# Hybrid decoder step: paced page gathers, one product for the rotary scores, four row groups for the mLSTM outer products, another start and end

## The reference

```
h = RMSNorm(x); z = h @ w_in
branch A: gated DeltaNet, 4 heads, chunked, state S per sample
branch B: latent attention, 8 heads; a sample reads 2048 past rows
          (128 latent + 32 rotary values) from pages of a page table:
          s = (q_lat . c_past + q_rope . k_past) * scale; softmax; ctx = p . c_past
branch C: mLSTM, 4 heads, chunked; C = decay * C + w * k (outer) v per sample
x += w_out(sum_b sigmoid(gate_b) * (o_b @ w_branch_b))
x += ConvFFN(RMSNorm(x)); after the last layer y = RMSNorm(x)
```

## Time and profile before

| what | value |
|---|---|
| median of 3 runs | 1277.28 us (1276.53 to 1277.31) |
| the profiled execution, its own time | 1287.18 us |
| its span, first to last instruction | 1285.3 us |
| mean granted clock of TensorE | 0.995 |
| busy: PE, PEld | 1258.9 us (98%), 1027.3 us (80%) |
| busy: DVE, ACT, POOL | 546.0 (42%), 254.3 (20%), 153.1 (12%) |
| chain that ended last | PE 93%, DVE 3%, issue 2%, ACT 1% |
| matmuls of L547 in it | 75% |
| DMA | 194.30 MB, mean 151 GB/s |
| TensorE waited for DVE, L1553 (start) | 6.7 us, once |
| for ACT, L1167, ahead of L1039 | 6.3 us, twice |
| for DVE, L1894, ahead of L833 | 2.5 us, twice |
| for DVE, L1510 (end) | 1.5 us, once |

### The profile page before, as it was taken

One profiled execution on the slowest core, in us unless ns is written; L12 is line 12 of the kernel. 1 busy time (PEld: TensorE's weight loads), 2 busy tenths in 40 slices (PEclk: granted clock), 3 DMA queues, 4 the chain that ended last, 5 costly groups with the idle time before them and its releaser, 6 DMA issues.

```text
span 1285.3 us, 18245 instructions
## 1 busy us (share of the span) xinstructions
PE 1258.9 (98%) x7278; PEld 1027.3 (80%) x7278; DVE 546.0 (42%) x1372; ACT 254.3 (20%) x648; POOL 153.1 (12%) x210
## 2 busy tenths in 40 slices
PE   7999999999999999999999999999999999999997
PEld 6878777677888888888888787786788888888885
DVE  7975646332135333331178846553311353334212
ACT  3432325222000111110033224342210011111000
POOL 2012442200000000020001035412000000000000
PEclk9999999999999999999999999999999999999999
DMA  9433476522444444464444344745234444444440
GB/s 336 153 99 102 132 249 226 214 82 83 132 153 147 148 148 148 147 218 151 147 152 137 109 129 145 259 164 213 67 99 147 152 145 149 149 149 148 153 133 34
DMA packets 59603, 194.30 MB, mean 151 GB/s; under 512 B 7824, under 2 KB 8112, under 8 KB 56704
## 3 DMA queue, kind: packets, MB, share of 16 engines
q1 hardware_dynamic: 50544, 152.22, 36.6%
q0 software_dynamic: 8768, 40.84, 8.9%
q10 hardware_dynamic: 208, 0.09, 0.0%
HBM read 183.86 MB, written 9.25 MB: 150 GB/s over the span
## 4 chain that ended last, share of the span: by engine, by line
PE 93%; DVE 3%; issue 2%; ACT 1%; POOL 0%; another core or an unknown queue 0%; DMA 0%; ACTq 0%; DVEq 0%; POOLq 0%
PE banks L547 75%; PE banks L1032 3%; PE banks L1039 1%; PE banks L1042 1%; PE banks L938 1%; PE banks L1078 1%; DVE arena L1658 1%; PE banks L966 1%; PE banks L691 1%; PE banks L847 0%; PE banks L982 0%; PE banks L564 0%; DMA arena<-in_par 0%; POOL arena L2282 0%
## 5 line engine op out<-in xcount | busy, mean ns | idle before, releaser
L547 PE MATMUL banks<-arena 128*128 128x264 f32 x4512 | 1032.1, 388 | 7.4 <-DVE arena L1553 6.7
L547 PEld LDWEIGHTS banks<-arena 128*128 128x128 f32 x4512 | 850.7, 190 | 171.8 <-issue 14.3
L1167 ACT ACTIVATE arena<-banks 128x256 f32<-128x256 f32 (+8 forms) x260 | 96.9, 397 | 436.0 <-PE banks L547 293.6
L2153 DVE TENSOR_SCALAR arena<-arena 128x256 f32<-128x256 f32 x44 | 18.2, 414 | 129.9 <-ACT arena L1167 129.7
L2186 DVE SCALAR_TENSOR_TENSOR arena<-banks,arena 128x264 f32<-128x264 f32 x16 | 6.9, 433 | 135.0 <-PE banks L547 135.0
L2364 POOL COPY arena<-arena 128x2 f32<-128x2 f32 x44 | 13.6, 310 | 377.7 <-ACT arena L1167 276.0
L1747 DVE SCALAR_TENSOR_TENSOR arena<-arena,banks 128x264 f32<-128x264 f32 x16 | 6.9, 430 | 73.6 <-PE banks L547 73.6
L1198 ACT ACTIVATE arena<-banks 128x264 f32<-128x264 f32 x32 | 12.5, 391 | 127.4 <-PE banks L547 127.4
L1032 PEld LDWEIGHTS banks<-arena 128*128 128x128 f32 x256 | 28.8, 145 | 7.4 <-issue 7.3
L2052 DVE COPY arena<-banks 128x512 f32<-128x512 f32 x32 | 21.5, 679 | 28.5 <-PE banks L1032 15.7
L1032 PE MATMUL banks<-arena 128*128 128x128 f32 x256 | 32.1, 280 | 0.0
(11 more groups left out here) (435 smaller groups left out, 1042.9 us busy)
## 6 DMA issues: line engine op xcount, KB each, us to landing
arena<-in_weights SPq DMA_DIRECT2D x230, 512.0 KB, 3.5
arena<-in_weights SPq DMA_DIRECT2D x112, 256.0 KB, 3.0
arena<-in_s POOLq DMA_DIRECT2D x2, 2048.0 KB, 11.0
out_ss_o<-arena POOLq DMA_DIRECT2D x16, 256.0 KB, 3.0
arena<-in_mla_w POOLq DMA_DIRECT2D x4, 1024.0 KB, 6.8
arena<-in_c POOLq DMA_DIRECT2D x4, 512.0 KB, 5.8
out_sc_o<-arena POOLq DMA_DIRECT2D x16, 128.0 KB, 3.5
arena<-in_x SPq DMA_DIRECT2D x4, 264.0 KB, 5.2
```

The source lines that it names most:

```text
L547: mm = nc.tensor.matmul(dst, ring[:, at_:at_ + 128], rhs[:, j, :], start=(start and j == 0), stop=(stop and j == k - 1))
L1167: return A(dst, src, ACT.Copy, scale=scale)
L2153: link(ts(cv, fc[:, j % 3, 0:TP], w[0], par[:, Q_FB + j:Q_FB + j + 1], ALU.mult, ALU.add))
```

## The change

Six edits. (1) Gathers: sequence 4 is gathered as before; sequence n = 5, 6, 7 only after TensorE has finished the transposes of sequence n - 4. (2) The rotary weights are one 128 x 128 block-diagonal block for each g and s, and one matmul takes the place of four. (3) The transposes of `kwpad` and `mvpad` are each followed by a plain matmul with the identity that writes the same rows into partitions 64 to 127, `kvt` and `vd` are copied with 128 partitions, and the four mLSTM outer products use row groups 0 to 3. (4) One more filler ahead of mn0, `half(2)` for `half(1)` in `schedule()` and in TensorE's and ScalarE's streams, `half(7)` for `half(6)` in VectorE's; one less in the last stretch. (5) Start: x's first part is loaded from ScalarE's queue, the first unit of weights in two halves with a signal for the first, x's second part between them, and the `prow` loads have their own signal. (6) End: the sums of squares are taken by token on three columns (256 tokens and the last 128, of which 8 count), the last tile's squares go to TensorE unsummed; root and reciprocal work on 128 x 3; TensorE spreads the result to two banks; VectorE makes tiles 0 to 4 from one, ScalarE copies the other to SBUF and POOL makes tiles 5 to 7 of it; ScalarE's queue stores those. The scaling by the norm's weights moves ahead, to each last tile.

```diff
@@ schedule
-    add("mkT", 2); add("mvT", 2); add("sk", 1, "V"); add("mqk", 2, "V"); add("os", 1, "V"); half(1)
+    add("mkT", 2); add("mvT", 2); add("sk", 1, "V"); add("mqk", 2, "V"); add("os", 1, "V"); half(2)
@@ sync
             sp.dma_start(par, a["par"][0]).then_inc(*up("par_loaded", 16))
-            load_x(0)
...
                 if u == 1:
-                    for i in range(1, 4):
+                    for i in range(2, 4):
                         load_x(i)
...
+                    if u == 0 and at_ == 0:
+                        sp.dma_start(ring[:, 0:512], units[h // 2][:, 512 * (h % 2):512 * (h % 2) + 512]).then_inc(first_half, 16)
+                        load_x(1)
+                        continue
...
+            for k, n in ((0, 2), (2, 2), (4, 1)):
+                sp.wait_ge(last_norm, k + n)
+                sp.dma_start(a["y"][:, TT * k:TT * (k + n)], hn[:, k:k + n, :].rearrange("p k n -> p (k n)")).then_inc(y_out, 16)
@@ tensor
-                        if part == 0:
+                        if unit == 0 and part == 0:
+                            pe.wait_ge(first_half, 16)
+                        elif part == 0 or unit == 0 and part == 4:
                             pe.wait_ge(w_landed[slot], landed[unit])
...
-                nc.tensor.transpose(b[0:64, 0:P], kwpad.rearrange("p t n -> p (t n)"), ident).then_inc(out_ready, 1)
+                nc.tensor.transpose(b[0:64, 0:P], kwpad.rearrange("p t n -> p (t n)"), ident)
+                nc.tensor.matmul(b[64:128, 0:P], kwpad.rearrange("p t n -> p (t n)"), ident, start=True, stop=True,
+                                 skip_group_check=True).then_inc(out_ready, 1)
...
-                    nc.tensor.matmul(b, kvt[32 * t:32 * t + 32, :], vd[32 * t:32 * t + 32, 4 * part:4 * part + 4, :].rearrange("p n v -> p (n v)"),
+                    nc.tensor.matmul(b, kvt[32 * j:32 * j + 32, :], vd[32 * j:32 * j + 32, 4 * part:4 * part + 4, :].rearrange("p n v -> p (n v)"),
...
-                    for i in range(4):
-                        mm = nc.tensor.matmul(sb[32 * i:32 * i + 32, :], qr_pad[:, i, g, s_, :], krt[:, n % 2, :],
-                                              start=False, stop=(s_ == 3), skip_group_check=True)
+                    mm = nc.tensor.matmul(sb, qr_pad[:, g, s_, :], krt[:, n % 2, :], start=False, stop=(s_ == 3), skip_group_check=True)
...
-            pe.wait_ge(last_sum, 7)
-            nc.tensor.matmul(banks[:, 0, 0:TT], ones, nsum, start=True, stop=True).then_inc(last_total, 1)
+            tokens = [slice(0, P), slice(P, TP), slice(TT - P, TT)]
+            pe.wait_ge(last_sum, 6)
+            for i, s in enumerate(tokens):
+                nc.tensor.matmul(totals[:, i:i + 1], nsum[:, s], ones[:, 0:1], start=(i == 0), stop=False, skip_group_check=True)
+            pe.wait_ge(last_square, KT)
+            for i, s in enumerate(tokens):
+                mm = nc.tensor.matmul(totals[:, i:i + 1], nsquare[:, 1, s], ones[:, 0:1], start=False, stop=True, skip_group_check=True)
+            mm.then_inc(last_total, 1)
+            pe.wait_ge(last_inverse, 1)
+            for b in last_rms:
+                for i, s in enumerate(tokens[:2]):
+                    nc.tensor.matmul(b[:, s], roots[:, i:i + 1].to_broadcast((P, P)), ident, start=True, stop=True, skip_group_check=True)
+                nc.tensor.matmul(b[:, TP:TT], roots[96:128, 2:3].to_broadcast((32, P)), ident[96:128, P - NB:P],
+                                 start=True, stop=True, skip_group_check=True).then_inc(last_spread, 1)
@@ scalar
+            nc.scalar.dma_start(x[:, 0:2, :].rearrange("p k n -> p (k n)"), a["x"][:, 0:2 * TT]).then_inc(x_in[0], 16)
             act.wait_ge(rows_clear, 1)
...
-            A(rms, banks[:, 0, 0:TT], ACT.Sqrt, scale=1.0 / D, bias=EPS).then_inc(last_root, 1)
+            A(roots, totals, ACT.Sqrt, scale=1.0 / D, bias=EPS).then_inc(last_root, 1)
+            act.wait_ge(last_spread, 2)
+            A(rms, last_rms[1], ACT.Copy).then_inc(last_copy, 1)
@@ vector
-            dve.wait_ge(*at(0, "par_loaded", 80))
+            dve.wait_ge(*at(0, "par_loaded", 16))
...
-                        at_ = i * 256 + P * g
-                        last = V.tensor_copy(arena[32 * i:32 * i + 32, qr_at + at_:qr_at + at_ + 160].rearrange("p (s m) -> p s m", s=4)[:, :, 0:8],
+                        at_ = qr_at + 512 * g + 32 * i
+                        last = V.tensor_copy(arena[32 * i:32 * i + 32, at_:at_ + 544].rearrange("p (s m) -> p s m", s=4)[:, :, 0:8],
...
-            V.reciprocal(rms, rms).then_inc(last_norm, 1)
...
+            V.reciprocal(roots, roots).then_inc(last_inverse, 1)
+            dve.wait_ge(last_spread, 1)
+            for k in range(5):
+                tt_(hn[:, k, :], raw[:, k, :], last_rms[0], ALU.mult).then_inc(last_norm, 1)
@@ gpsimd
-                for n in range(4, NB):
+                gather(4)
+                for n in range(5, NB):
+                    pool.wait_ge(*out(l, "ltr", 4 * (n - 4) + 3))
+                    plain()
                     gather(n)
...
+            for k in range(5, KT):
+                tt_(hn[:, k, :], raw[:, k, :], rms, ALU.mult).then_inc(last_pool, 1)
```

More of the change, by code:

```diff
@@ L404, in build @@
             i, j = STREAM[2 * (u % UNITS)], STREAM[2 * (u % UNITS) + 1]
-            runs.append([(i, 0, 2)] if i % 2 == 0 and j == i + 1 else [(i, 0, 1), (j, 1, 1)])
-            total[u % SLOTS] += 16 * len(runs[-1])
+            runs.append([(i, 0, 2)] if u and i % 2 == 0 and j == i + 1 else [(i, 0, 1), (j, 1, 1)])
+            total[u % SLOTS] += 16 * len(runs[-1]) if u else 16
             landed.append(total[u % SLOTS])
-        w_started = sem("w_started")
+        w_started, first_half = sem("w_started"), sem("first_half")
         out_ready = sem("out_ready")
@@ L418, in build @@
         last_square, last_root, last_norm, y_out = sem("last_square"), sem("last_root"), sem("last_norm"), sem("y_out")
+        last_inverse, last_spread, last_copy, last_scaled, last_pool = (
+            sem(f"last_{n}") for n in ("inverse", "spread", "copy", "scaled", "pool"))
         rows_clear = sem("rows_clear")
@@ L454, in bank @@
             return banks[:, BANK_OF[name, i], :]
+        roots, totals = cols[:, 0:3], bank("fd", 0)[:, 0:3]
+        last_rms = [bank("fd", i)[:, 0:TT] for i in (1, 2)]
         def slot(j):
@@ L827, in _ @@
                 nc.tensor.matmul(heads(b[:, 0:NS], NB), vnew, vsel, start=True, stop=True).then_inc(out_ready, 1)
-                half(1)
+                half(2)
                 pe.wait_ge(*at(l, "ones_column", 1))
@@ L890, in _ @@
                 plain()
[L891 removed]
+                nc.tensor.transpose(b[0:64, 0:P], kwpad.rearrange("p t n -> p (t n)"), ident)
+                nc.tensor.matmul(b[64:128, 0:P], kwpad.rearrange("p t n -> p (t n)"), ident, start=True, stop=True,
+                                 skip_group_check=True).then_inc(out_ready, 1)
                 b = claim("mvvT")
                 plain()
[L894 removed]
+                nc.tensor.transpose(b[0:64, 0:P], mvpad.rearrange("p t n -> p (t n)"), ident)
+                nc.tensor.matmul(b[64:128, 0:P], mvpad.rearrange("p t n -> p (t n)"), ident, start=True, stop=True,
+                                 skip_group_check=True).then_inc(out_ready, 1)
                 half(2)
@@ L1347, in _ @@
                 act.wait_ge(*out(l, "out", 7))
-                copy(kvt[0:64, :], bank("mkvT")[0:64, 0:P]).then_inc(*read("mkvT"))
+                copy(kvt, bank("mkvT")[:, 0:P]).then_inc(*read("mkvT"))
                 half(3)
@@ L1502, in norm_part @@
                 V.tensor_tensor(nsquare[:, k % 2, :] if k else nsum, x[:, k, :], x[:, k, :], ALU.mult).then_inc(*square_of(None))
-                if first is not None:
+                if first is None:
+                    ts(raw[:, k, :], x[:, k, :], par[:, Q_NF + k:Q_NF + k + 1], None, ALU.mult).then_inc(last_scaled, 1)
+                    if k == KT - 1:
+                        return
+                else:
                     ts(raw[:, k, :], x[:, k, :], par[:, (Q_N2 if first else Q_N1) + k:(Q_N2 if first else Q_N1) + k + 1], None,
@@ L1901, in _ @@
                 V.tensor_copy(windows[:, :, 0:232:33], mq[:, :, TP:TT])
-                half(6)
+                half(7)
                 dve.wait_ge(*at(l, "s_decayed", 8))
@@ L1941, in _ @@
                 dve.wait_ge(*out(l, "out", 7))
-                tt_(vd[0:64], bank("mvvT")[0:64, 0:P].unsqueeze(1).to_broadcast((64, NB, P)), eighth[0:64].unsqueeze(2).to_broadcast((64, NB, P)),
+                tt_(vd, bank("mvvT")[:, 0:P].unsqueeze(1).to_broadcast((P, NB, P)), eighth.unsqueeze(2).to_broadcast((P, NB, P)),
                     ALU.mult).then_inc(*up("mv_diag"))
@@ L2195, in _ @@
             dve.wait_ge(last_root, 1)
-            V.reciprocal(rms, rms).then_inc(last_norm, 1)
-            dve.wait_ge(last_norm, 1)
-            for k in range(KT):
```

(5 more changed lines are left out.)

25 lines of the change are left out of this document (14 added, 11 removed).

## The result

The changed kernel takes 1279.59 us (median of 17 runs) against 1277.28 before it: 1.002 times as long, 95% interval 1.0012 to 1.0028. It is slower by 2.3 us, where 6.4 us were forecast to be gained and the range ended at 1274.5. One run of the 17, in a slow state with a granted clock of 0.848 where the others had 0.995 to 0.997, took 1465.34 us and is left out of the comparison.

What follows compares the result with a forecast made beforehand. TensorE, mostly its weight passes, bounds the kernel. The terms sum to -16.0 us for the profiled execution (1271.2); without the gathers' 9.6 the timed runs go from 1277.28 by -6.4 to 1270.9, range 1260 to 1274.5.

Steps and rivals of the forecast that it cites:

- gathers, in the timed runs: Page loops: pacing the late gathers saves 9.6 us in the profiled execution but nothing in the timed runs.
- filler ahead of mn0: Half a tile more fills TensorE's 1.23 us wait ahead of mn0: -1.7 us a layer, -3.4 in all.
- outer products: mLSTM: four row groups shorten the products, but VectorE holds mq and two new matmuls cost time: +0.3 us.
- rotary scores: Page loop: one full matmul for four column-tiled ones, -0.02 us for each of 16, -0.3 us in all.
- head: Start: x's second part arrives sooner, moving TensorE's ones product from 13.23 to about 12.0: -1.2 us.
- tail: Behind the last projection: shorter norm chain, products shared by VectorE and POOL, last product at 1280.9 for 1282.8: -1.8 us.
- the 9.6 us: Time lost between pages 0 and 3 in both layers' page loops, 4.8 to 4.9 us each, in the profiled execution.
- the hole: TensorE's wait in each layer's page loop, 3.16 us in layer 0, while four late gathers issued in one burst run.
- Rival 1: Page loops: the hole is in the timed runs too, so they fall by 16.0 us to 1261.3; chance 0.33.
- VectorE's long product: Ahead of mn0: VectorE's 4.66 us product beside POOL's, over at 152.02, stays covered as TensorE needs it at 152.9.
- the new wait at mq: Behind the mLSTM outer products: TensorE waits some 0.6 us before mq for VectorE's four additions.
- Rival 4: Page loop: paced transfers delay a count on every page, 1.6 us for each of 8 pages: 1283.7 us; chance 0.04.

Runs made afterwards that it cites:

- experiment 5: Kernel before the change with only its page gathers paced as in the change: 1277.11 us against 1277.16.
- experiment 7: Kernel before the change with only the extra half slab of filler ahead of mn0 in each layer: 1273.51 us, 3.65 less than before.
- experiment 3: Changed kernel with the mLSTM sample outer products as they were (one transpose each, two row groups, 64 partitions): 1277.60 us, 2.0 less than the changed kernel.
- experiment 4: Changed kernel with the rotary scores again as four matmuls of 32 weight columns on four column groups: 1278.71 us, 0.9 less than the changed kernel.
- experiment 6: Kernel before the change with only the change's head (split first weights, x's first quarter from ScalarE, parameter rows counted apart): 1276.73 us, 0.4 less.
- experiment 8: Changed kernel with last products on VectorE and outer products and rotary scores as before: 1272.31 us, 7.3 faster than the changed kernel.
- experiment 2: Kernel before the change with one wait more: GpSimd waits for VectorE's last product before it closes. 1280.99 us, ratio to before 1.0029.
- experiment 1: Changed kernel with its last three products on VectorE instead of GpSimd, without the second spread and ScalarE's copy: 1275.41 us, 4.2 less than the changed kernel.
- experiment 9: Kernel of experiment 8 with its last stores in two pairs from SyncE, not three from SyncE and ScalarE: 1271.66 us, 0.65 less.
- experiment 10: Kernel of experiment 8 with the column halves and 128-partition copy and diagonal back, outer products in two row groups: 1274.81 us, 2.5 more.

## Why the prediction was wrong

**By its terms.** The measured size is a difference of medians, of the changed kernel and the one without the part, or of before and before with the part:

| term | forecast | measured | by |
|---|---|---|---|
| gathers, in the timed runs | 0 | -0.05 | experiment 5 |
| filler ahead of mn0 | -3.4 | -3.65 | experiment 7 |
| outer products | +0.3 | +2.0 | experiment 3 |
| rotary scores | -0.3 | +0.9 | experiment 4 |
| head | -1.2 | -0.4 | experiment 6 |
| tail | -1.8 | +3.5 | what is left of +2.3 |
| sum | -6.4 | +2.3 | |

**Gathers.** The choice was right: the 9.6 us were in one profiled execution and not in the runs. The three profiles with the burst and without the hole show it, and so does experiment 5. Rival 1, to which I gave 0.33, was wrong. That the recording made the hole, as I argued, is not shown, and the spans of the 67 timed runs speak against it.

**Filler.** Right in place and size: the second outer products took up the shift, and VectorE's long product stayed covered.

**Tail.** This is the step that failed: "the last product ends at 1280.9 in place of 1282.8", with the end 2.5 us behind it as before. The chain up to the products was right in the main: with VectorE doing them all, the last is over 1.6 us sooner (experiment 8). But the 2.5 us held only as long as the last work was VectorE's and the last store SyncE's. I moved three products to GpSimd and did not ask what GpSimd does when it is done. Its DRAIN of 5.87 us holds the end back by 3.6 us (1277.02 against SyncE's 1273.40); the wait alone cost 3.8 us in experiment 2, and the products' move to GpSimd 4.2 us in experiment 1, the longer way to the last of them included. The Trainium skill ("VectorE: DVE Perf Modes", "The DRAIN you can't avoid") has the closing DRAINs at a constant of about 12 ns on all five engines; the trace agrees for SyncE's (7 ns), and disagrees by far for GpSimd's (5867 ns). By positions: the last product is over 6.9 us behind the last projection, where 5.9 were forecast (GpSimd starts 0.6 later, and its three products take 2.14 us, where 3 x 0.57 were estimated) and 7.8 were taken before; and the program ends 6.1 us behind it, in place of 2.5. That makes -0.9 + 3.6 = +2.7. The medians leave +3.5 for the tail, a remainder of five differences. Of the other 0.8 us, 0.2 lie outside the span: a run takes 2.1 us more than its span in the three kernels whose last products are GpSimd's, and 1.8 to 1.9 in all others. What the rest is no run shows.

**Outer products.** The step was "four passes of 0.11 (half of 0.223), which cost 0.2 to 0.44": 1.05 by the rows, and 2.0 us in all, beyond the bound of +0.8. The passes themselves are as short as that, but at each change into or out of the upper column half, four a layer, TensorE stands for a moment. The first pair starts 0.21 us apart, where two transposes start 0.11 apart, and the next transpose comes 0.36 us later. It is not the change between a transpose and a plain matmul as such: in experiment 8 a plain pass is followed by the first transpose after 0.22 us and the second transpose by a plain pass after 0.11, with nothing lost. The weight load of the second half is not put ahead, as others are; TensorE's weight loads of the changed kernel:
```profile
172.33 0.11 PEld L901 LDWEIGHTS banks<-arena 128*64 128x64 f32 x1
172.75 0.19 PEld L902 LDWEIGHTS banks<-arena 128*64 128x64 f32 x2 [0.31 <-issue]
```
It starts with its matmul, at 172.75, and so do the loads at the other three changes, the last of them that of the full weights at 173.71. The trace of before has no such pair, and I took the passes alone for the bound. The other half of the part, the new wait at mq, was right.

**Rotary scores.** Inside the bounds and with the wrong sign, by the positions at least: the nearest row gave the pass, but not the load in front of it. The prediction says that the trace of before has no full load right behind column-tiled passes. It has one on most pages: the transposes' first load of 128 x 128, at 247.09 in the earlier trace rows, starts with its pass and 0.5 us behind the last rotary pass, where the column-tiled ones follow each other after 0.41 to 0.45.

**Head.** The size was off by a wait for x's third part, which appears only once the second is sooner. The -0.4 is itself not told from zero; the positions say -0.6.

**Rivals.** None of the four is what happened. Rival 4, the only slower one, put the danger into the gathers, where the range left it out. The danger lay in the part that I called a gain with bounds of one sign (-0.8 to -2.6), though it gave work to an engine that had been done for 80 us.

## What to carry to other kernels

An engine whose last work lies far ahead of the end may have a close of its own that nobody sees. Before giving it a part in the tail, read its single records behind its last instruction, here 5.87 us of DRAIN on GpSimd, and keep it out of the last 6 us; even one wait there brings it back. A change of several parts is worth undoing one by one: here three pieces that cost 7.3 us together hid a gain of 4.9, most of it the filler's. And where a profiled execution is longer than the runs by just the hole that one wants to close, a second profile of the same work settles it.

## What the runs showed of the hardware that was not expected

- GpSimd's closing DRAIN took 5867 ns in the kernel before and in experiments 1, 2 and 5 to 10 alike, whether it stood behind the waits at the end of its work or behind one wait for VectorE; behind products, in the changed kernel and in experiments 3 and 4, it ended 5.89 us after the last of them. SyncE's took 7 ns.
- A transpose of 64 columns of weights followed by a matmul of the same tile into the other column half: 0.27 and 0.43 us, started 0.21 and 0.36 apart, where two transposes one behind the other start 0.11 apart. Going back from the upper half to full weights opens the load too (0.36 us from the last pair to the next weights, two passes of 0.11 in it); going from plain passes to transposes in the lower half and back costs nothing.
- A full weight load behind column-tiled passes of 512 columns cost 0.1 us once; four loads of 32 columns cost nothing there.
